# Weighing every eighth expert row of a gathered mixture on VectorE instead of TensorE

## What is computed

```
h = h + peer(rmsnorm(h, peer_norm_g), peer_w_q, peer_sub_keys, peer_u, peer_v)
return rmsnorm(h, final_norm_g)
```

## Time and profile before

| | before |
|---|---|
| median of 3 runs | 2616.47 us (2616.11 to 2616.98) |
| span of the profiled execution, first to last instruction | 2610.4 us |
| TensorE matmul, busy | 2315.4 us (89%) |
| VectorE, busy | 1432.9 us (55%) |
| ScalarE, busy | 682.3 us (26%) |
| GpSimd, busy | 606.6 us (23%) |
| chain that ended last | TensorE 55%, DMA 32%, VectorE 8% |
| HBM read | 651.48 MB |

### The profile page before, as it was taken

One profiled execution on the slowest core, in us unless ns is written; L12 is line 12 of the kernel. 1 busy time (PEld: TensorE's weight loads), 2 busy tenths in 40 slices (PEclk: granted clock), 3 DMA queues, 4 the chain that ended last, 5 costly groups with the idle time before them and its releaser, 6 DMA issues.

```text
span 2610.4 us, 23382 instructions
## 1 busy us (share of the span) xinstructions
PE 2315.4 (89%) x7780; PEld 1235.5 (47%) x7780; DVE 1432.9 (55%) x3734; ACT 682.3 (26%) x1633; POOL 606.6 (23%) x566
## 2 busy tenths in 40 slices
PE   7999999999999989899988998898878878788886
PEld 3456554456554465458644444444334333343332
DVE  0010332055540966421776777787777677677775
ACT  2010013126320145412343222233222232222222
POOL 0002000010000000000244434445434444344441
PEclk8999999999999989999999999999999999999989
DMA  8101423100112100140699999999999999999996
GB/s 339 65 33 65 194 101 125 37 28 1 40 65 97 69 33 33 36 175 33 251 406 393 415 421 422 421 411 421 421 421 421 422 421 421 423 421 421 422 421 274
DMA packets 83798, 655.09 MB, mean 251 GB/s; under 512 B 9394, under 2 KB 9682, under 8 KB 11362
## 3 DMA queue, kind: packets, MB, share of 16 engines
q0 software_dynamic: 75760, 549.07, 50.9%
q1 hardware_dynamic: 7922, 104.55, 10.3%
HBM read 651.48 MB, written 2.10 MB: 250 GB/s over the span
## 4 chain that ended last, share of the span: by engine, by line
PE 55%; DMA 32%; DVE 8%; issue 2%; ACT 2%; POOL 0%; SPq 0%; DVEq 0%; POOLq 0%; ACTq 0%; PEldq 0%
DMA arena<-in_peer_uv,newton 30%; PE psum L596 21%; PE psum L1232 10%; PE psum L682 3%; PE psum L1108 2%; DVE arena L2305 2%; DMA arena<-in_weights 2%; PE psum L1173 1%; PE psum L836 1%; PE psum L890 1%; PE psum L1044 1%; DVE arena L2283 1%; PE psum L1201 1%; DVE small L2284 1%; PE psum L844 1%
## 5 line engine op out<-in xcount | busy, mean ns | idle before, releaser
L1232 PE MATMUL psum<-arena 128*128 128x512 f32 x2048 | 966.6, 620 | 212.3 <-ACT arena L1635 209.6
L2305 DVE CUSTOM_DVE_ANT_0 arena<-arena 128x1024 f32<-128x1024 f32 x512 | 620.8, 1224 | 283.6 <-DMA arena<-in_peer_uv,newton 279.9
L2465 POOL DMA_INDIRECT arena<-in_peer_uv,newton x512 | 564.3, 1102 | 834.7 <-PE psum L1232 709.9
L1232 PEld LDWEIGHTS psum<-arena 128*128 128x128 f32 x2048 | 394.0, 198 | 696.4 <-issue 691.8
L596 PE MATMUL psum<-arena 128*128 128x512 f32 (+2 forms) x1440 | 551.2, 544 | 10.6 <-ACT arena L1385 5.2
L596 PEld LDWEIGHTS psum<-arena 128*128 128x128 f32 (+1 forms) x1440 | 271.1, 189 | 287.8 <-issue 276.6
L1317 ACT ACTIVATE arena<-psum 128x512 f32<-128x512 f32 (+10 forms) x316 | 167.3, 546 | 661.4 <-PE psum L596 306.9
L1635 ACT ACTIVATE arena<-ident,newton 128x128 f32<-128x128 f32 x512 | 177.8, 394 | 266.6 <-DVE newton L2314 264.5
L1626 ACT ACTIVATE arena<-arena 128x2 f32<-128x2 f32 (+1 forms) x258 | 52.5, 203 | 659.3 <-DVE arena L2305 659.2
L1201 PE MATMUL psum<-arena 128*128 128x256 f32 x480 | 122.3, 380 | 1.9 <-DMA arena<-in_weights 1.5
L1201 PEld LDWEIGHTS psum<-arena 128*128 128x128 f32 x480 | 91.0, 190 | 63.2 <-issue 54.4
(11 more groups left out here) (318 smaller groups left out, 2034.2 us busy)
## 6 DMA issues: line engine op xcount, KB each, us to landing
arena<-in_weights SPq DMA_DIRECT2D x47, 2048.0 KB, 8.6
arena<-in_peer_uv,newton POOLq DMA_INDIRECT x512, 24.9
arena<-in_xin SPq DMA_DIRECT2D x1, 3072.0 KB, 27.8
arena<-in_fnet_w POOLq DMA_DIRECT2D x1, 2048.0 KB, 20.1
arena<-in_cmp_w POOLq DMA_DIRECT2D x1, 2048.0 KB, 7.5
out<-arena SPq DMA_DIRECT2D x4, 512.0 KB, 11.8
arena<-in_pool_band POOLq DMA_DIRECT2D x1, 1280.0 KB, 9.7
arena<-in_dft_l POOLq DMA_DIRECT2D x1, 1028.0 KB, 12.1
```

The source lines that it names most:

```text
L1232: ins = mm(bank(j_y[t][q]), DIAG[i % 4], ROW[ROW_PLACE[i]][:, D + 512 * q:D + 512 * q + 512], start=first, stop=last)
L2305: v.tensor_tensor_reduce(out=u, in0=u, in1=HNT[ITEM_TILE[i // 16]][:, :], scale=1.0, scalar=0.0, op0=ALU.mult, op1=ALU.add, accum_out=DOTS ...
L2465: g.indirect_dma_start(out=ROW[ROW_PLACE[i]][:, :], out_offset=None, in_=a["peer_uv"], in_offset=bass.IndirectOffsetOnAxis(ap=IDX[:, n, e: ...
```

## The change

Rows with `i % 8 == 4` up to row 492 (`VECTOR_ROWS`, 62 of 512) no longer pass through ScalarE's diagonal and TensorE. VectorE adds `gate * v` to `HTT[t]` in one instruction over all 1024 columns, right after the `weigh` of their batch. Such a row is always the first of its batch, in batches q = 2 and q = 6 of an item. The last 16 rows stay as they were. GpSimd waits for such a row's buffer on a new semaphore `row_added`; the counters of `row_used` and `diag_ready` skip these rows.

```diff
+VECTOR_ROWS = [i for i in range(N_ROWS - 16) if i % 8 == 4]
+MATMUL_COUNT = [sum(k not in VECTOR_ROWS for k in range(i + 1)) for i in range(N_ROWS)]
+VECTOR_COUNT = [sum(k in VECTOR_ROWS for k in range(i + 1)) for i in range(N_ROWS)]
...
                 for i in BATCHES[b]:
+                    if i in VECTOR_ROWS:
+                        continue
...
-                    pe.wait_ge(S["diag_ready"], i + 1)
+                    pe.wait_ge(S["diag_ready"], MATMUL_COUNT[i])
                     for q in range(2):
-                        ins = mm(bank(j_y[t][q]), DIAG[i % 4], ROW[ROW_PLACE[i]][:, D + 512 * q:D + 512 * q + 512],
+                        ins = mm(bank(j_y[t][q]), DIAG[(MATMUL_COUNT[i] - 1) % 4], ROW[ROW_PLACE[i]][:, D + 512 * q:D + 512 * q + 512],
...
                 for i in BATCHES[b]:
-                    if i >= 4:
-                        act.wait_ge(S["row_used"], i - 3)
+                    if i in VECTOR_ROWS:
+                        continue
+                    if MATMUL_COUNT[i] > 4:
+                        act.wait_ge(S["row_used"], MATMUL_COUNT[i] - 4)
                     n, e = divmod(i, 16)
-                    fn(DIAG[i % 4], ident[:, :], ACT.Copy, scale=GATES[:, n, e:e + 1]).then_inc(S["diag_ready"], 1)
+                    fn(DIAG[(MATMUL_COUNT[i] - 1) % 4], ident[:, :], ACT.Copy, scale=GATES[:, n, e:e + 1]).then_inc(S["diag_ready"], 1)
...
                 v.tensor_tensor(gate, gate, DOTS[:, i:i + k], ALU.mult).then_inc(S["wgt_ready"], 1)
+                for r in BATCHES[b]:
+                    if r in VECTOR_ROWS:
+                        t, c = ITEM_TILE[r // 16], VECTOR_COUNT[r]
+                        dve.wait_ge(S["wgt_ready"], b + 1)
+                        if c > 1:
+                            dve.wait_ge(S["row_added"], c - 1)
+                        v.scalar_tensor_tensor(out=HTT[t][:, :], in0=ROW[ROW_PLACE[r]][:, D:2 * D],
+                                               scalar=GATES[:, n, r % 16:r % 16 + 1], in1=HTT[t][:, :],
+                                               op0=ALU.mult, op1=ALU.add).then_inc(S["row_added"], 1)
...
             def add_y(t):
+                dve.wait_ge(S["row_added"], max(VECTOR_COUNT[16 * n + 15] for n in range(ITEMS) if ITEM_TILE[n] == t))
...
                 full(dve, j_y[3][q])
+                dve.wait_ge(S["row_added"], len(VECTOR_ROWS))
...
                 if ROW_BEFORE[i] is not None:
-                    pool.wait_ge(S["row_used"], ROW_BEFORE[i] + 1)
+                    if ROW_BEFORE[i] in VECTOR_ROWS:
+                        pool.wait_ge(S["row_added"], VECTOR_COUNT[ROW_BEFORE[i]])
+                    else:
+                        pool.wait_ge(S["row_used"], MATMUL_COUNT[ROW_BEFORE[i]])
```

More of the change, by code:

```diff
@@ L369, in build @@
             gelu_done wgt_ready diag_ready y_full y_free fin_sq fin_sqrt fin_ready
-            out_stored pq_full pq_used mem_o_used xb_ready chunks_summed last_sum last_sq last_root last_gain sgu_biased ug_biased row_used p_exp cmp_shifted mask_loaded""".split()
+            out_stored pq_full pq_used mem_o_used xb_ready chunks_summed last_sum last_sq last_root last_gain sgu_biased ug_biased row_used row_added p_exp cmp_shifted mask_loaded""".split()
         S = {n: sem(n) for n in names}
```

## The result

| | before | after |
|---|---|---|
| median of 20 runs each | 2614.20 us (2612.13 to 2619.41) | 2618.76 us (2615.52 to 2621.83) |
| ratio | | 1.0015, 95% interval 1.0009 to 1.0022 |
| span of the profiled execution | 2610.4 us | 2618.1 us |

The change costs 3.9 us (0.15%) between the means of the runs and 4.6 us between their medians. It stays inside what was called "within 0.2%" and inside the range, but the sign is the other one: 1.4 us less was forecast. More runs make the difference clear of chance. They also correct a number of the prediction: the later runs of before give their spans beside their times, and the time is 2.3 us above the span (1.8 us for the change), so the profiled execution of before took some 2612.7 us and the three runs of 2616.5 us were slower than most, not 6.1 us of work outside the span.

A forecast was written before the change was run, and what follows sets the result against it. Transfers at 421 GB/s were taken to bound the kernel. With 7 buffers, 2.4 us of relief against 1.0 us of delay gave -1.4, so 2616.5 - 1.4 = 2615.1 us; range 2609.5 to 2620.5 us.

The forecast's parts named there:

- within 0.2%: Whole kernel: no measurable change, since measurement resolves about 0.2%, 5.2 us; chance 0.79.
- The ceiling: Any gain at most 9.3 us: 7.7 with 7 buffers, 1.6 with 9, nothing with 14.
- Three signs: TensorE's busy time down about 100 us, landing times longer in late stages, last gather issued within 3 us of before.
- The sum there: Stretch of 7 buffers: gain from earlier buffers less loss from later dots, net -1.4 us.
- The delay: Window with TensorE full, 7 buffers: added instructions make following dots late, half counted, 1.0 us.
- The relief: Window with TensorE full, 7 buffers: removed matmuls release buffers earlier, worth 2.4 us.
- The clock: Stretch of 7 buffers: TensorE's granted clock falling with more pauses; nothing counted for it in the sum.
- rival 3: Stretch of 7 buffers: TensorE pauses more, clock drops; four more pauses at about 1.6 us give 2621.5 us; chance 0.03.
- Rival 2: Stretch of 7 buffers: added VectorE instruction delays next dots and transfers, at most 12.2 us, to 2628.7 us; chance 0.05.
- Rival 1: Stretch of 7 buffers: earlier buffers close all gaps, 7.7 to 9.3 us faster, 2607 to 2609 us; chance 0.12.
- Rival 4: Added instruction holds up GpSimd's gathers and stops transfers, up to 79 us, to 2696 us; chance 0.01.
- The sign that was to tell them apart: Below 400 GB/s between 1270 and 1450 us: VectorE full means rival 2, low clock means rival 3.

The follow-up runs named there:

- e10_later_rows: The change for rows 70 to 492 alone (53 rows), the earlier ones as in the kernel before: +0.9 +- 0.8 us against before, ratio 1.0005.
- e8: The kernel before plus sixteen VectorE instructions of factor 0.0 among the first 70 rows, all rows still through TensorE: +4.6 +- 0.8 us against before.
- e14: The kernel before plus 33 VectorE instructions of factor 0.0 in the first 70 rows: +9.2 +- 1.5 us against before, ratio 1.0034.
- e13: The change with sixteen rows below 70, neither multiplied nor added, TensorE products with zeros in place of their matmuls: -2.3 +- 0.7 us against before.
- e7: The change with sixteen rows below 70, neither multiplied nor added (left out of the output): -0.2 +- 0.6 us against before, ratio 1.0001.
- e1: The change, with TensorE also multiplying zeros after each batch with a vector row, as many matmuls as removed: +1.9 +- 0.8 us against before.
- e4: The change for its nine rows below row 70 alone: +1.9 +- 0.6 us against before, ratio 1.0009.
- e5: The change with sixteen vector rows, all below row 70, none later: +3.8 +- 1.0 us against before, ratio 1.0012.
- e3: The change without its VectorE instruction, the 62 value rows added nowhere: +2.7 +- 0.7 us against before, ratio 1.0010.

## Why the prediction was right and wrong

**Right: where it can matter.** The ceiling was read from the rates, and the stages of 9 and 14 buffers did hide the change: 419 and 421 GB/s in e10_later_rows at a clock of 0.93 and 0.89. That is why 62 rows moved from one engine to another change the time by 0.15%. The price of the instruction (1.29 us), VectorE's busy time (up by 77 us) and the idle time that it fills (72 us of an expected 80) were as expected. Three signs failed. TensorE's busy time fell by 52 us and not by 100, for the clock. The landing time in the stage of 14 buffers did not grow: its median was 26.6 us and is 26.4. The last gather was issued 8.8 us later in the first profile of the change (2578.7 against 2569.9 us) and 2.9 us later in the second.

That the time fell inside the range is in part luck. The range hung on 2616.5 us for before, 2.3 us above the median of twenty runs; counted from before it reaches from -7.0 to +4.0 us, and the change costs 3.9.

**Wrong: "The sum there".** Three terms failed, all in the stretch of 7 buffers.

- *The delay*, "1.4 x 1.36 / 2 = 1.0 us" was charged in the one window where TensorE was full, for 1.4 of the nine rows. It falls due wherever the queue is short, which is the whole stretch: 0.29 us an instruction (e8, e14), 2.6 us for nine. That is 21% of each 1.36 us, less than the half assumed, but for nine rows. The step that failed is to count a delay only where the other engine was full; VectorE's being late needs no help from TensorE.
- *The relief*, 2.4 us, came to 2.3 us for sixteen rows at a held clock (e13), so about 1.3 us for nine.
- *The clock* was put at nothing in the sum and made rival 3 with a chance of 0.03, on the argument that four more pauses would be needed. Taking an eighth of TensorE's rows lowered the clock there from 0.96 to 0.91, in both profiles of the change. That costs 2.2 us for sixteen rows (e13 against e7), so about 1.2 for nine if it goes by their number, and 2.0 +- 1.0 in the whole change (e1 against it).

For nine rows: 2.6 - 1.3 + 1.2 = +2.5 us, against +1.9 +- 0.6 measured (e4), and +3.9 for all 62. The clock was as low with nine rows (0.92 in e4) as with sixteen (0.91 in e5), so its term may not go by their number; with 2.0 the sum is +3.3. The rest, if it is not chance, is with the later rows, though in the profiles the time from gather 70 on is the same within 2 us. One number stays unexplained: by these terms relief and clock nearly cancel, as they do in e7 (-0.2 +- 0.6), but e3, with nine early rows and 53 later ones skipped, cost +2.7 +- 0.7. In the stretch of 7 buffers the relief was to outweigh the delay, and it is half of it, before the clock takes it away.

**The rivals.** Rival 2 was the nearest in mechanism (VectorE's delay), with a price that was its ceiling: of 12.2 us a fifth arrives. Rival 3's mechanism is at work with it. Rival 1 is excluded: even the relief alone for sixteen rows gives 2.3 of its 7.7 us. Rival 4 is excluded at its price of 79 us; what may be left to it is 1.6 +- 1.0 us for sixteen rows. The chances had treated 2 and 3 as alternatives to a small gain, while they are terms of one sum with it, each present with a fraction. The sign that was to tell them apart misled: under 400 GB/s, VectorE not full (137 of 180 us) and the clock low (0.91) pointed to rival 3, while the larger term is the delay. VectorE need not be full for a late dot to cost time.

## What to carry to other kernels

When a stage waits for transfers, look for the stretch in which the queue is shortest and make the sum for that stretch alone, with every added instruction charged at some fraction (here a fifth), not only where another engine is full. Work taken from TensorE isn't free time: if the pauses get longer the granted clock falls, and the rest of its work takes longer; check the mean duration of the matmuls that stay. Where the effect is below what two profiles of one kernel differ by, double the dose in the stretch that matters and take the terms apart (add only, skip only, filler) in many runs.

## What the runs showed that was not expected

- Removing work can slow a kernel: e3_skip_only, +2.7 +- 0.7 us, though sixteen early rows alone (e7) did not. The mean granted clock of a whole execution went from 0.965 (mean of 33 runs of before) to 0.942 in the change and 0.943 in e3; two rows' matmuls took 6.59 us, most of it at 1.2 GHz, where they take 3.67 at 2.4. What TensorE did before was wait for a diagonal, 3.59 us; after 1.92 us of waiting at the same place they took 3.67. The Trainium skill, "TensorE: Matmul & The Clock Gate", section "HAM oscillation — how this bites in real kernels", has the rule that waits for transfers between bursts of matmuls send TensorE back to its lower clock; the trace agrees, for waits for a diagonal, which itself waits for a landed row: in the stretch of 7 buffers the mean clock fell by 0.05 with an eighth less of these rows.
- Products of a zero matrix hold the clock up as real ones do: 0.98 with them (e1), 0.91 without (the change), at the same useful work.
- The time at which the stage begins varies by up to 4.4 us between executions whose instructions up to there are the same (first gather at 1263.8 us in before, 1266.0 in its repetition, 1268.2 in e5), more than the change costs.
